# Attention on one Trainium2 core: in every odd step, half of the projection part moves between scores and transposes

## The reference

```
xn = rms_norm(x, g_pre_mix)
z  = xn @ w_in                                  # q | k | v | conv | pool | gates
q, k: 8 heads x 2 components x 64;  v: 8 heads x 128
for each block of 128 queries (8 blocks), for each head, for each component c of 2:
    sc = (q_c * 64**-0.5) @ k_c^T, causal
    p_c = softmax(sc)
p_diff = p_0 - lam * p_1
y = rms_norm(p_diff @ v, subln_g) * (1 - lambda_init)
```

## Time and profile before

| | us |
|---|---|
| median of 3 runs (1784.74 to 1785.03) | 1785.0 |
| the profiled execution | 1785.24 |
| its span | 1783.7 |

### The profile page before, as it was taken

The page is one execution under the profiler, slowest core; times in us unless marked ns, Lnnn a source line. Parts: engine busy times, 40 slices in busy tenths (PEclk is TensorE's granted clock), DMA queues, the critical chain, the costliest instruction groups (busy, mean ns, idle before and its releaser), DMA issues. The chain is left out here.

```text
span 1783.7 us, 25018 instructions
## 1 busy us (share of the span) xinstructions
PE 1758.8 (99%) x8496; PEld 1456.0 (82%) x8496; DVE 1145.8 (64%) x1850; ACT 735.3 (41%) x1477; POOL 251.1 (14%) x558
## 2 busy tenths in 40 slices
PE   7999999999999999999999999999999999999998
PEld 6888888888878888888888888888888888888886
DVE  4328999899875765451365655686665655567666
ACT  4216666666743333342122223343333333334553
POOL 3221222222110001112100102101001100000011
PEclk9999999999999999999999999999999999999999
DMA  7321222222132223326735722323322322683443
GB/s 252 135 91 48 72 72 71 71 71 71 53 137 83 80 68 106 112 95 215 263 118 165 247 71 84 105 95 112 118 94 106 123 89 88 220 292 95 144 142 128
DMA packets 139256, 214.21 MB, mean 120 GB/s; under 512 B 7632, under 2 KB 95184, under 8 KB 138144
## 3 DMA queue, kind: packets, MB, share of 16 engines
q1 hardware_dynamic: 110384, 109.06, 19.4%
q0 software_dynamic: 28784, 104.04, 16.0%
HBM read 150.69 MB, written 62.39 MB: 119 GB/s over the span
## 5 line engine op out<-in xcount | busy, mean ns | idle before, releaser
L2693 PE MATMUL ps<-d_op 128*128 128x512 f32 x924 | 210.3, 389 | 0.1
L2693 PEld LDWEIGHTS ps<-d_op 128*128 128x128 f32 x924 | 173.3, 188 | 36.8 <-DVE d_op L1547 0.5
L2637 PE MATMUL ps<-s_op,t_op_T 128*128 128x512 f32 x720 | 169.9, 389 | 0.0
L2390 PE MATMUL ps<-xn,ring 128*128 128x512 f32 x672 | 166.9, 398 | 0.0
L2637 PEld LDWEIGHTS ps<-s_op,t_op_T 128*128 128x128 f32 x720 | 135.2, 188 | 28.0
L2390 PEld LDWEIGHTS ps<-xn,ring 128*128 128x128 f32 x672 | 122.5, 188 | 24.1
L2503 PE MATMUL ps<-s_op,x_op_T 128*128 128x512 f32 x540 | 127.4, 389 | 0.0
L2503 PEld LDWEIGHTS ps<-s_op,x_op_T 128*128 128x128 f32 x540 | 101.4, 188 | 21.0
L2637 PE MATMUL ps<-hn,t_op_B 128*128 128x512 f32 x480 | 115.1, 389 | 0.0
L2637 PEld LDWEIGHTS ps<-hn,t_op_B 128*128 128x128 f32 x480 | 90.1, 188 | 18.7
L1069 ACT ACTIVATE e_t<-ps,neg_max 128x256 f32<-128x256 f32 (+7 forms) x128 | 94.0, 740 | 15.6 <-DVE neg_max L1651 14.1
(11 more groups left out here) (263 smaller groups left out, 3384.5 us busy)
## 6 DMA issues: line engine op xcount, KB each, us to landing
pair<-in_w_gate_up_dram SPq DMA_DIRECT2D x20, 1024.0 KB, 5.1
rf_pieces<-s_scratch SPq DMA_DIRECT2D x74, 256.0 KB, 2.7
x_pair<-in_w_in_dram SPq DMA_DIRECT2D x15, 1024.0 KB, 6.2
raw<-in_w_in_dram SPq DMA_DIRECT2D x28, 512.0 KB, 4.0
s_scratch<-gated_ff POOLq DMA_DIRECT2D x40, 256.0 KB, 2.4
gate_in<-gate_scratch POOLq DMA_DIRECT2D x18, 512.0 KB, 3.6
v_scratch<-v_out POOLq DMA_DIRECT2D x32, 256.0 KB, 2.6
vh<-v_scratch POOLq DMA_DIRECT2D x16, 512.0 KB, 5.2
```

The source lines that it names most:

```text
L2390: last = pe.matmul(ps[:, proj_bank(first, half), :], proj_weights(which, par, a)[:, P * k:P * (k + 1)], xn[:, b, k, HALF * half:HALF * (ha ...
L2637: last = pe.matmul(ps[:, bank, :], t_op[name][:, a, k, :], block(b, k), start=opens and (k, a, b) == (0, HH, HH), stop=(k, a, b) == (3, LL ...
L2693: last = pe.matmul(ps[:, DOWN_BANKS[product][i], :], d_op[:, g % 4, a, P * i:P * (i + 1)], d_op[:, g % 4, 2 + b, :], start=opens and (a, b ...
```

## The change

In every odd step i (all heads), the first 6 of the 12 projection matmuls move from behind the transposes of the difference to the place between scores and transposes. The other 6 stay behind the transposes. Step 0 is as before. Since `proj_part` is now called twice for odd parts, its signal `proj_done` and its counter step are given by the second call alone (`piece[1] == 4`).

```
-                if part % 2 == 1:
+                if part % 2 == 1 and piece[1] == 4:
                     last.then_inc(proj_done, 1)
                     p.next()
...
-                ahead = 2 if not lag and i == 0 and not first else 0
+
+                ahead = 2 if not lag and (i % 2 == 1 or i == 0 and not first) else 0
                 if ahead:
-                    proj_part(0, 0, 1 - par, piece=(0, ahead))
+                    proj_part(i // 4, i % 4, 1 - par, piece=(0, ahead))
```

## The result

| kernel | median us | runs | ratio to before, 95% interval |
|---|---|---|---|
| before | 1784.87 | 1784.71 to 1785.03 | |
| changed | 1807.51 | 1806.13 to 1809.58 | 1.0130, 1.0118 to 1.0142 |

The changed kernel is 22.6 us slower. Forecast were 1804.6 and a range of 1794 to 1815. The profiled execution took 1806.13, its span is 1804.5, so the two traces differ by 20.8 us. From the first scores of the attention stage to the transposes behind the last head it is 129.20 to 504.51 now and 130.32 to 483.55 before: 375.3 instead of 353.2 us, 22.1 more. The stage starts 1.1 us earlier in the second trace, and what follows differs by 0.1. So all of the loss lies in the attention stage.

A forecast was written before the change was run, and what follows sets the result against it. PE was taken as the bound, busy 1758.8 of 1783.7 us, in a chain through ACT and nearly full DVE. Terms 1.6 + 8.75 + 3.2 + 4.0 + 1.0 + 1.0 = 19.6 on 1785.0 gave 1804.6, range 1794 to 1815.

The forecast's parts named there:

- Switches: PE in each of 32 odd steps: one more switch between matmuls and transposes, 0.05 us a step, 1.6 us in all.
- Step 7 into 0: Seven places: late pt copies delay exponentials and qt, so PE waits in the next head's step 0; 1.25 us each, 8.75.
- Step 5 into 6: Eight places: delayed exponentials make the difference late for PE's transposes in step 6; 0.5 us each, 4.0, bounds 0.2 and 0.9.
- what costs nothing: Parts of the attention stage put at no cost, among them weighted values and the result's transpose sharing bank 5.
- Step 3 into 4: Eight places: difference and low part of kt come late for PE in step 4; 0.4 us each, 3.2.
- First head: Step 2 of the first head, where PE already waits 0.8 us for kt: 1.0 us more, bounds 0.5 and 1.5.
- Last head: Behind the last head, PE's wait of 1.0 us for the last difference grows by 1.0, bounds 0.5 and 1.4.
- only step 0 pays: Rival: DVE's spare 10% swallows what steps 3 and 5 pass on; 11.3 us slower, 1796.3; chance 15%.
- every step pays in full: Rival: delays do not fit in DVE's spare time, every odd step pays; 45 us slower, 1830; chance 8%.
- hidden: Rival: the delay is hidden and the change only adds switches; 1.6 us slower, 1786.6; chance 6%.
- faster: Rival: projection matmuls load under the last scores where transposes can't; 8 us faster, 1777; chance 5%.
- Slower by the clock: Rival: each new wait brings ten slow matmuls behind it; 24 waits add 40 us, 1844; chance 4%.

The follow-up runs named there:

- only7: Kernel before with only step 7 changed (half of its projection ahead of the transposes); steps 1, 3, 5 as before: 1791.16 us, ratio 1.0043.
- exp_first_old: Kernel before, PE's order untouched, with ACT in odd steps making the first exponential ahead of the pt copies: 1796.85 us, ratio 1.0070.
- ylo_early: Changed kernel, with DVE in step 5 making the low part of y_out ahead of that of qt instead of last: 1803.34 us, ratio 1.0106.
- only1: Kernel before with only step 1 changed: 1787.46 us, ratio 1.0019.
- only5: Kernel before with only step 5 changed: 1790.72 us, ratio 1.0035.
- only13: Kernel before with only steps 1 and 3 changed: 1789.64 us, ratio 1.0031.
- exp_first: Changed kernel, with ACT in odd steps making the first exponential ahead of the pt copies: 1795.89 us, ratio 1.0068.
- ahead1: Changed kernel with 3 projection matmuls instead of 6 ahead of the transposes in odd steps: 1791.02 us, ratio 1.0037.
- tail_old: Kernel before; behind the last head, the last difference's 8 transposes stand behind the first 6 of the next job's 24 matmuls: 1782.67 us, ratio 0.9990.
- tail2_old: As tail_old, with the transpose of the very last result also moved behind the next 24 projection matmuls: 1779.53 us, ratio 0.9973.

## Why the prediction was right, and what it mis-sized

The time was within the range and 2.9 us above the forecast (22.6 us more than before instead of 19.6). The chain from late transposes over ACT to PE is the one that was forecast. That the sum came so close is in part luck: a wait that was not forecast added 3.0 us, and 0.9 us that the loop's jumps had cost before went under the new waits. By its steps:

- **Switches**, 0.05 a step: measured 0.09, 0.09, 0.08 and 0.07 in steps 1, 3, 5 and 7, so 2.6 us in 32 steps instead of 1.6. Six matmuls take 1.50 behind scores and 1.47 behind transposes, a little more than the 1.49 and 1.45 that step 0 had shown.
- **Step 7 into 0**, 1.25: measured 0.88 in step 0 and 0.24 at the end of step 7, 1.12. The mechanism is that of the text, and the stall comes in two pieces, as it said. It is shown by only7, and by exp_first_old, which makes the same stall from ACT's side. The two copies hand over after 0.87 us (264.76 to 265.63), not the 0.98 of their duration, which explains 0.1.
- **Step 5 into 6**, 0.5: measured 0.70 in step 6 and 0.28 at the end of step 5, 0.98, above the upper bound of 0.9. This is the term that was mis-sized most, by a wait and not by the forecast chain. The chain gives what was forecast: 0.28 for exponentials, and 0.23 before the transposes, which start 1.65 behind the start of the scores (254.04 to 255.69) instead of 1.42, for the difference comes late. But the last two of the six transposes write bank 5, in which the transpose of the last result lies until DVE has made the low part of `y_out`, and DVE does that last in its step. The prediction had looked at bank 5 in one direction only (result's transpose behind those of the difference) and put it under "what costs nothing". ylo_early shows the share: 0.40 of the transposes' 1.11, 0.4 a head and 3.0 us in all.
- **Step 3 into 4**, 0.4: measured 0.35 and 0.20, 0.55. 0.3 of it is there already when step 1 alone is changed (only1), and the prediction had put step 1 at nothing. It had taken DVE's idle time in step 1 for slack, but most of that is a wait of 0.54 us for POOL that is over before the delay arrives: only1 has it too (0.55), and the 0.62 for exponentials behind it. What step 3 would cost by itself no run shows.
- **First head**: forecast 1.0 more in step 2, measured 0.26 more from the scores to the transposes and 0.58 more in the wait for `kt`, 0.84. **Last head**: 1.0 at its end, measured 1.93 instead of 1.04. In the last head itself, what steps 3 and 5 hand on was put at 0.9 and took 0.6, the waits at the ends of these steps included. DVE has no low part of `qt` or `kt` to make there, which may be why; no run shows it.
- **Loop turns**, not in the prediction: before, two heads take 44.57 and 44.73 instead of 44.19. They are those behind the two jumps back of the loop, where DVE idles 1.56 and 1.73 us. After the change these heads take 47.14, like the others: the jump is hidden under waits. That is 0.9 us that the change does not cost.
- **The rivals**: "only step 0 pays" fell by only5 and only13; "every step pays in full" was far off; "hidden" and "faster" fell by the first waits read. What "faster" hoped for did not come either: where projection matmuls stand behind the scores, it is their loads that are held back, 8.1 us in 19 places against 1.1 in one before, while those of the transposes fell from 10.2 to 6.2; the sum has risen from 11.3 to 14.3. "Slower by the clock" is not what cost the 22.6 us: the granted clock is 1.00 in the loop, with waits of up to 0.8 us, and it fell in the changed kernel's trace only behind the wait of 2.48 us after the stage, as it does in the trace of before. But the prediction's reason against it, that waits of 1.0 and 0.8 us leave the clock alone, does not reach to 1.34 us, as only13 shows.

The four runs of the changed kernel lie 3.5 us apart, those before 0.3. The granted clock, which is on record for each run as its mean, goes with it: 0.998 in the two runs of 1806.1 and 1806.5, 0.997 at 1808.5 and 0.996 at 1809.6. A thousandth of 1800 us is 1.8 us. Where the clock fell in the runs that have no trace stays open.

## What to carry to other kernels

Before work is put ahead of a hand-over, ask who stands behind that hand-over in the receiving engine's queue: ACT's exponentials had nothing to do with the transposes, and were held up for 1.2 us because their copies stood first. Work moved ahead of a wait pays only where the wait exists; here it existed at two places behind the loop, worth 4.9 us with what the clock gave back, and at none in it. Slack is to be measured at the last consumer of each buffer, in both directions, and a delay that fits in a nearly full engine is not gone but arrives some steps later.

## What the hardware showed that was not expected

The granted clock falls for a moment behind some waits of PE and not behind others of the same length. In only7, PE waited 1.97 us behind the last head; busy time of PE, granted clock, DMA share and GB/s in stretches of 2 us:

```profile
488.00:490.00 2.00, 1.10 (x10) 1.00 0.00 0
490.00:492.00 2.00, 0.93 (x5) 0.71 0.00 0
492.00:494.00 2.00, 2.00 (x8) 0.50 0.01 4
494.00:496.00 2.00, 2.00 (x9) 0.94 0.00 0
496.00:498.00 2.00, 2.00 (x10) 1.00 0.30 79
```

0.50 is the level of 1.2 GHz. In only13 the same came behind a wait of 1.34 us for `kt` in step 2 of the first head:

```profile
138.00:140.00 2.00, 0.53 (x4) 1.00 0.04 8
140.00:142.00 2.00, 1.93 (x7) 0.78 0.34 100
142.00:144.00 2.00, 2.00 (x6) 0.50 0.54 163
144.00:146.00 2.00, 2.00 (x11) 0.86 0.03 11
```

Step 2 takes 7.50 us there. It takes 5.89 in only1 and 5.90 in the changed kernel, which have the same wait of 1.34 us and a clock of 1.00 behind it. So this fall cost 1.6 us, on top of the wait.

| wait of PE, us | clock behind it fell in | clock stayed at 1.00 in |
|---|---|---|
| 0.7 to 1.31 | no trace | all twelve |
| 1.34, first head | only13 | changed, only1, ylo_early |
| 1.72, behind the last head | exp_first_old | exp_first |
| 1.93 to 1.97, behind the last head | only7 | changed, ylo_early |
| 2.48 to 2.50, last result | before (0.90 from 510 to 520), changed (0.83 from 530 to 540), only7, only1, ahead1, exp_first, ylo_early | only5, only13, exp_first_old, tail_old |

tail2_old, which has no wait of over 1.02 us from the stage on, stays at 1.00 from 480 to 530. So in this kernel the price of a wait was its length, and from 1.34 us on sometimes more on top of it. Which executions it meets, the traces do not tell. That this is why executions of one kernel differ by 1 to 4 us is borne out by the mean clock on record for each run: only7 takes 1790.8 to 1791.2 us in the three runs with 0.999, and 1794.2 and 1794.9 in the two with 0.997.
